# Chunk attention in pairs of heads, with matmuls on alternating row and column halves of TensorE

## The chip, the cores and the metric

The kernel runs on one core of one Trainium2 chip. The metric is the device time of one execution in microseconds (us); lower is better. The time of the kernel before is the median of three executions. A profile of one further execution is what is read below.

## The reference

The reference is a streaming encoder trunk of two layers over 512 tokens of width 1024: an S5/DeltaNet mixer, cross-attention and a SwiGLU network in layer 0; a chunk attention, cross-attention and SwiGLU in layer 1. The change touches the chunk attention alone:

```python
def chunk_attention(h, w_qkv, w_out, q_g, k_g, rel_bias):     # 16 heads of 64, CHUNK = 64
    qkv = (h @ w_qkv).reshape(bsz, seq, 3, CA_HEADS, CA_HEAD_DIM)
    q, k, v = rms_norm(qkv[:, :, 0], q_g), rms_norm(qkv[:, :, 1], k_g), qkv[:, :, 2]
    ...
    def one_chunk(c):      # 64 queries against their own chunk and the 8 chunks before it
        s = jnp.einsum('bqhd,bkhd->bhqk', q_c, k_c) * scale + bias     # bias: learned, by distance
        s = jnp.where((band_pos + start) >= 0, s, -1e30)
        p = jax.nn.softmax(s, axis=-1)
        return jnp.einsum('bhqk,bkhd->bqhd', p, v_c)
    ...
    return o @ w_out
```

With 512 tokens the band covers everything before a query, so it is attention that is causal by chunks of 64.

## The kernel before

One hand-written instruction stream per engine; semaphores alone order them. Tokens lie in four tiles of 128 rows (TT = 4, P = 128). The large products take each f32 operand as a high and a low part (three matmuls, lines 310 to 312); chunk attention itself works on plain f32. One f32 matmul of the program appears in the trace as two matmul instructions; a transpose appears as one.

Query and key are held transposed (`cqT`, `ckT`) with two heads to a 128-row block: head h lies in rows 64*(h % 2) to 64*(h % 2) + 63 of block h // 2. Head by head, for the four row blocks i of queries with n = 128*(i + 1) keys each (1280 columns a head):

- **scores** (`ca_scores_pe`, L1763): a matmul on 64 rows of the array, into PSUM bank i;
- **sums** (in `ca_dve`, L1846): DVE adds the bias from a ring of four tiles (`bias_ring`, loaded by `ca_sp`), writes `p_c` and takes the row maximum; L1850 negates the maxima. L1840 first writes -1e30 into a 64x64 corner of the bias tile (the mask);
- **exps** (L1823): ACT exponentiates the four row blocks with their sums;
- **rescale** (L1861, L1864): DVE takes the reciprocals of the sums and scales the four row blocks;
- **turn** (`ca_turn_p_pe`, L1773): TensorE transposes p, key block s of all row blocks into one of the three PSUM banks 4 to 6 in rotation, ten transposes a head;
- **copy** (`ca_copy`): out of those banks into `pT_c`; s = 0 and 3 by ACT (L1795), s = 1 and 2 by DVE (L1797);
- **values** (`ca_values_pe`, L1782): v times p transposed into 64 partitions (a column half of the array) of bank 7;
- **out_hi, out_lo** (L1833 on ACT, L1855 on DVE): bank 7 split into the high and low part of the output, 64 partitions each.

TensorE's order is turn(h), scores(h + 2), values(h); DVE's is out_lo(h - 1), two copies, rescale(h + 1), sums(h + 2); ACT's is two copies, exps(h + 1), out_hi(h). After the last out_lo comes the output projection (L310). In the code below `link` and `after` are helpers that count semaphores.

Of the kernel before, what the change touches and what calls it, by code (L numbers as in the profile page):

```python
# [5 lines left out]
F32 = mybir.dt.float32  # L6
# [5 lines left out]
P = 128  # L12
# [58 lines left out]
def build_program(nc, A):  # L71
    ctx = ExitStack()
    with ctx:
# [9 lines left out]
        with nc.sbuf_tensor("params", [P, N_PAR], F32) as par:  # L83
# [999 lines left out]
        LEVELS = 5  # L1083

        def solve_start_pool(g):

            for i in range(TT):
# [589 lines left out]
        c_max, c_neg, c_sum, c_rec = cs(2, TT), cs(2, TT), cs(2, TT), cs(2, TT)  # L1677
        ck_rows = rows(high_b)
        cqT, ckT = feat(high_c), feat(high_d)
        p_c = [reg(arena + 2048 * n, TT, SEQ) for n in range(2)]  # L1680
        pT_c = [reg(at_b + 2048 * n, TT, SEQ) for n in range(2)]
        c_oT = hT


# [69 lines left out]
        def ca_scores_pe(pe, h):
            r = slice(64 * (h % 2), 64 * (h % 2) + 64)
            if h == 0:
# [8 lines left out]
        def ca_turn_p_pe(pe, h):  # L1765
            for s in range(TT):
                m = 4 * h + s
                if m >= 3:
                    pe.wait_ge(sem(COPY[(m - 3) % 4][0]), 2 * ((m - 3) // 4) + COPY[(m - 3) % 4][1])
# [6 lines left out]
        def ca_values_pe(pe, h):
            r = slice(64 * (h % 2), 64 * (h % 2) + 64)
            if h > 0:
                pe.wait_ge(sem("c_ol"), h)
            for s in range(TT):  # L1780
                pe.wait_ge(sem(COPY[s][0]), 2 * h + COPY[s][1])
                ins = pe.matmul(ps[r, 7, s * P:SEQ], v_rows[:, s, h * CD:(h + 1) * CD], pT_c[h % 2][:, s, s * P:SEQ],  # L1782
                                start=(s == 0), stop=(s == TT - 1), skip_group_check=True)
            ins.then_inc(sem("c_o"), 1)


        COPY = [("c_pa", 1), ("c_pv", 1), ("c_pv", 2), ("c_pa", 2)]

        def ca_copy(eng, h, s):
            eng.wait_ge(sem("c_tr"), 4 * h + s + 1)  # L1790
            if h >= 2:
                eng.wait_ge(sem("c_o"), h - 1)
            dst, src = pT_c[h % 2][:, s, s * P:SEQ], ps[:, 4 + (4 * h + s) % 3, s * P:SEQ]
            if COPY[s][0] == "c_pa":
                eng.activation(dst, src, ACT.Copy).then_inc(sem("c_pa"), 1)  # L1795
            else:
                eng.tensor_copy(dst, src).then_inc(sem("c_pv"), 1)  # L1797

        def ca_pe(pe):

            ca_scores_pe(pe, 0)
            ca_scores_pe(pe, 1)
            for h in range(CH):
                ca_turn_p_pe(pe, h)
                if h + 2 < CH:
                    ca_scores_pe(pe, h + 2)
                ca_values_pe(pe, h)

        def ca_sp(sp, h):
            if h == 0:  # L1810
                sp.wait_ge(sem("c_rows"), 1)
            if h >= 4:
                sp.wait_ge(sem("c_s2"), 4 * (h - 3))
            e = A["rel_rows"]
            src = bass.AP(e.tensor, h * BAND_E, [[1, P], [1, BAND_W]])
            sp.dma_start(bias_ring[:, h % 4, :], src).then_inc(sem(f"bias_in{h % 4}"), 16)

        def ca_act(a):
            def exps(h):
                a.wait_ge(sem("c_max"), h + 1)  # L1820
                for i in range(TT):
                    n = (i + 1) * P
                    a.activation(p_c[h % 2][:, i, 0:n], p_c[h % 2][:, i, 0:n], ACT.Exp, bias=c_neg[:, h % 2, i:i + 1],  # L1823
                                      accum_out=c_sum[:, h % 2, i:i + 1]).then_inc(sem("c_exp"), 1)
            exps(0)
            for h in range(CH):
                ca_copy(a, h, 0)
                ca_copy(a, h, 3)
                if h + 1 < CH:
                    exps(h + 1)  # L1830
                a.wait_ge(sem("c_o"), h + 1)
                r = slice(64 * (h % 2), 64 * (h % 2) + 64)
                a.activation(c_oT[0][r, h // 2, :].rearrange("p (i n) -> p i n", i=TT),  # L1833
                                  ps[r, 7, :].rearrange("p (i n) -> p i n", i=TT)[:, :, ::-1], ACT.Copy).then_inc(sem("c_oc"), 1)

        def ca_dve(v):
            def sums(h):
                v.wait_ge(sem(f"bias_in{h % 4}"), after(f"bias_in{h % 4}", 16 * (h // 4 + 1)))

                link(v, v.memset(bias_ring[64:P, h % 4, BAND_W - 64:BAND_W], -1e30), "dve_step")  # L1840
                if h >= 2:
                    v.wait_ge(sem("c_tr"), 4 * (h - 1))
                for i in range(TT):
                    n = (i + 1) * P
                    v.wait_ge(sem("c_s"), 4 * h + i + 1)
                    v.tensor_tensor_reduce(out=p_c[h % 2][:, i, 0:n], in0=ps[:, i, 0:n],  # L1846
                                                in1=bias_ring[:, h % 4, BAND_W - n:BAND_W], scale=1.0, scalar=-3.0e38,
                                                op0=ALU.add, op1=ALU.max, accum_out=c_max[:, h % 2, i:i + 1]).then_inc(sem("c_s2"), 1)
                v.wait_ge(sem("c_s2"), 4 * h + 4)
                v.tensor_scalar(c_neg[:, h % 2, :], c_max[:, h % 2, :], -1.0, None, ALU.mult).then_inc(sem("c_max"), 1)  # L1850

            def out_lo(h):
                r = slice(64 * (h % 2), 64 * (h % 2) + 64)
                v.wait_ge(sem("c_oc"), h + 1)
                v.tensor_tensor(c_oT[1][r, h // 2, :].rearrange("p (i n) -> p i n", i=TT),  # L1855
                                ps[r, 7, :].rearrange("p (i n) -> p i n", i=TT)[:, :, ::-1],
                                c_oT[0][r, h // 2, :].bitcast(F32).rearrange("p (i n) -> p i n", i=TT), ALU.subtract).then_inc(sem("c_ol"), 1)

            def rescale(h):
                v.wait_ge(sem("c_exp"), 4 * h + 4)  # L1860
                link(v, v.reciprocal(c_rec[:, h % 2, :], c_sum[:, h % 2, :]), "dve_step")  # L1861
                for i in range(TT):
                    n = (i + 1) * P
                    v.tensor_scalar(p_c[h % 2][:, i, 0:n], p_c[h % 2][:, i, 0:n], c_rec[:, h % 2, i:i + 1], None, ALU.mult).then_inc(sem("c_p"), 1)  # L1864
# [4 lines left out]
            for h in range(CH):
                if h > 0:  # L1870
                    out_lo(h - 1)
                ca_copy(v, h, 1)
                ca_copy(v, h, 2)
                if h + 1 < CH:
                    rescale(h + 1)
                if h + 2 < CH:
                    sums(h + 2)
            out_lo(CH - 1)
# [54 lines left out]
        def _(pe):  # L1933
# [37 lines left out]
            for l in range(DEPTH):  # L1971
# [153 lines left out]
        def _(g):  # L2125
# [78 lines left out]
```

## Time and profile before

| what | value |
|---|---|
| time, median of 3 runs (lowest to highest) | 1906.85 us (1906.24 to 1907.49) |
| the profiled execution: its own time / its span | 1907.66 us / 1905.9 us |
| mean granted TensorE clock, share of full | 0.96 |
| busy over the span: PE, DVE, ACT, POOL | 92%, 43%, 33%, 13% |
| the attention loop (1187.3 to 1297.2 us), busy: PE, DVE, ACT, POOL | 103.5, 79.4, 59.1, 0 of 109.9 us |
| TensorE instructions in that loop | 408 |

Instruction rows give a start, a duration, the engine (PE is TensorE, DVE VectorE, ACT ScalarE, POOL GpSimd), the line, the operation, what it writes and reads, shapes, and a count where rows are merged; in brackets stands the idle time before it and what ended it. A shape as 64*128 in a PE row is the rows and columns of the array in use. Matmuls are pipelined, so a merged row of n matmuls lasts from the first start to the last end, and the time of one is the distance between starts. The granted clock is 1.00 at 2.4 GHz and 0.50 at 1.2 GHz.

### The profile page before, as it was taken

The numbers are of one execution on the slowest core, as the hardware profiler recorded it, in microseconds if no ns is written. First come the engines' busy times: TensorE is split into PE (matmuls) and PEld (weight loads), VectorE is DVE, ScalarE is ACT, GpSimd is POOL, SyncE is SP. The second block draws the span as 40 slices with busy tenths as digits, with TensorE's granted clock in tenths as the row PEclk, the third lists the DMA queues.
The fourth block names the chain that finished last, engine by engine and source line by source line (L and its number), as shares of the span: only waits on it lengthen the run. The fifth ranks groups of instructions, "written<-read, shape, count | busy, mean of one in ns | idle before, by whom it ended". The sixth has DMA issues, their size and how long they took to land.

```text
span 1905.9 us, 20683 instructions
## 1 busy us (share of the span) xinstructions
PE 1762.2 (92%) x8392; PEld 1437.8 (75%) x8392; DVE 811.7 (43%) x1054; ACT 629.5 (33%) x998; POOL 238.8 (13%) x285
## 2 busy tenths in 40 slices
PE   6997585999998999999998999999998999999998
PEld 5877565987775788888887887557876778888887
DVE  5844554445535333333214353673545243333212
ACT  5222054224534333223114234453434233222210
POOL 1782003330000011111000000000000001111000
PEclk9997677999999999999999999899999999999999
DMA  6215001022420233332232231121431133333321
GB/s 197 89 39 95 0 1 45 1 67 88 155 89 23 66 84 92 89 109 88 97 102 89 75 120 53 37 72 45 162 104 44 48 86 88 97 101 88 105 94 67
DMA packets 146795, 151.97 MB, mean 80 GB/s; under 512 B 8864, under 2 KB 109344, under 8 KB 146592
## 3 DMA queue, kind: packets, MB, share of 16 engines
q1 hardware_dynamic: 146720, 150.92, 26.0%
q8 instruction: 53, 0.87, 0.2%
q14 instruction: 22, 0.18, 0.0%
HBM read 147.76 MB, written 3.15 MB: 79 GB/s over the span
## 4 chain that ended last, share of the span: by engine, by line
PE 85%; DVE 9%; ACT 3%; issue 2%; DMA 0%; POOL 0%; SPq 0%; DVEq 0%; ACTq 0%
PE ps L310 22%; PE ps L311 22%; PE ps L312 22%; PE ps L1763 2%; PE ps L1782 2%; PE ps L1504 2%; PE ps L1481 1%; PE ps L384 1%; PE ps L1121 1%; PE ps L1131 1%; PE ps L895 1%; PE ps L1136 1%; DVE sb L348 1%; PE ps L836 1%; PE ps L738 1%
## 5 line engine op out<-in xcount | busy, mean ns | idle before, releaser
L310 PE MATMUL ps<-h_hi,w_hi 128*128 128x512 f32 x864 | 337.2, 390 | 3.3 <-DVE w_lo_ab L282 3.3
L311 PE MATMUL ps<-h_lo,w_hi 128*128 128x512 f32 x864 | 336.8, 390 | 0.0
L282 DVE TENSOR_TENSOR w_lo<-raw,w_hi 128x2048 fp32r<-128x2048 f32 x70 | 160.4, 2292 | 408.1 <-ACT w_hi L278 408.1
L278 ACT ACTIVATE w_hi<-raw 128x2048 fp32r<-128x2048 f32 x84 | 160.6, 1913 | 430.6 <-PE ps L312 429.5
L312 PE MATMUL ps<-h_hi,w_lo 128*128 128x512 f32 x704 | 273.9, 389 | 0.0
L310 PE MATMUL ps<-w_hi,h_hi 128*128 128x512 f32 x512 | 199.8, 390 | 6.5 <-DVE h_lo L1557 2.8
L311 PE MATMUL ps<-w_lo,h_hi 128*128 128x512 f32 x512 | 199.2, 389 | 0.0
L312 PE MATMUL ps<-w_hi,h_lo 128*128 128x512 f32 x512 | 199.2, 389 | 0.0
L310 PEld LDWEIGHTS ps<-h_hi,w_hi 128*128 128x128 f32 x864 | 162.5, 188 | 37.6 <-DVE w_lo_ab L282 3.8
L311 PEld LDWEIGHTS ps<-h_lo,w_hi 128*128 128x128 f32 x864 | 162.6, 188 | 33.5
L1639 POOL CAST a_hi<-up 128x512 f32 x44 | 27.0, 614 | 1213.3 <-DVE up L1627 1213.3
L1629 DVE TENSOR_TENSOR w_lo<-raw,w_hi 128x2048 fp32r<-128x2048 f32 x44 | 140.6, 3194 | 52.2 <-ACT w_hi L1615 52.2
L312 PEld LDWEIGHTS ps<-h_hi,w_lo 128*128 128x128 f32 x704 | 132.2, 188 | 27.3
L1615 ACT ACTIVATE w_hi<-raw 128x2048 fp32r<-128x2048 f32 x44 | 84.4, 1918 | 197.2 <-PE ps L312 197.2
L1627 DVE TENSOR_TENSOR up<-up,ps 128x512 f32<-128x512 f32 x44 | 30.3, 688 | 262.3 <-PE ps L312 262.3
L310 PE MATMUL ps<-w_hi,a_hi 128*128 128x512 f32 x352 | 137.2, 390 | 1.8 <-DVE up L1627 1.8
L311 PE MATMUL ps<-w_lo,a_hi 128*128 128x512 f32 x352 | 136.9, 389 | 0.0
L312 PE MATMUL ps<-w_hi,a_lo 128*128 128x512 f32 x352 | 136.9, 389 | 0.0
L310 PEld LDWEIGHTS ps<-w_hi,h_hi 128*128 128x128 f32 x512 | 96.1, 188 | 28.8 <-DVE h_lo L1557 4.5
L312 PEld LDWEIGHTS ps<-w_hi,h_lo 128*128 128x128 f32 x512 | 96.1, 188 | 20.0
L311 PEld LDWEIGHTS ps<-w_lo,h_hi 128*128 128x128 f32 x512 | 96.1, 188 | 19.6
L310 PEld LDWEIGHTS ps<-w_hi,a_hi 128*128 128x128 f32 x352 | 66.1, 188 | 16.3 <-DVE up L1627 2.6
(331 smaller groups left out, 2551.7 us busy)
## 6 DMA issues: line engine op xcount, KB each, us to landing
raw<-in_f_w_gate SPq DMA_DIRECT2D x44, 512.0 KB, 4.0
raw<-in_f_w_up SPq DMA_DIRECT2D x44, 512.0 KB, 5.3
raw<-in_f_w_down SPq DMA_DIRECT2D x44, 512.0 KB, 4.2
raw<-in_xa_w_kv SPq DMA_DIRECT2D x16, 1024.0 KB, 5.0
raw<-in_c_w_qkv SPq DMA_DIRECT2D x12, 1024.0 KB, 5.0
raw<-in_ab_w_in SPq DMA_DIRECT2D x10, 1024.0 KB, 5.4
raw<-in_xa_w_q SPq DMA_DIRECT2D x8, 1024.0 KB, 5.0
raw<-in_xa_w_out SPq DMA_DIRECT2D x8, 1024.0 KB, 5.0
```

Source lines behind the costliest of these rows:

```text
L278: a.activation(w_hi[:, n % 2, :], raw[n % 2], ACT.Copy).then_inc(sem("w_hi"), 1)
L282: v.tensor_tensor(w_lo(n)[:, n % 2, :], raw[n % 2], w_hi[:, n % 2, :].bitcast(F32), ALU.subtract).then_inc(sem("w_lo"), 1)
L310: pe.matmul(out, a[0], b[0], start=start, stop=False)
L311: pe.matmul(out, a[0], b[1], start=False, stop=False)
L312: return pe.matmul(out, a[1], b[0], start=False, stop=stop)
L1504: ins = pe.matmul(ps[:, 6 + d, :], xv[:, s, h * XD + d * P:h * XD + (d + 1) * P], pT_x[h % 2][:, s, :], start=(s == 0), stop=(s == 1))
L1615: a.activation(w_hi[:, slot, :], raw[slot], ACT.Copy).then_inc(sem("w_hi"), 1)
L1627: v.tensor_tensor(prod[:, s, :], gsil[:, s, :], ps[:, 4 * s + 1, :], ALU.mult).then_inc(sem(f"f{l}_free"), 1)
L1629: v.tensor_tensor(w_lo(n0)[:, slot, :], raw[slot], w_hi[:, slot, :].bitcast(F32), ALU.subtract).then_inc(sem("w_lo"), 1)
L1639: g.tensor_copy(aT[0][:, at], prod[:, s, :]).then_inc(sem(f"f{l}_ahi"), 1)
L1763: pe.matmul(ps[:, i, 0:n], cqT[r, h // 2, i * P:(i + 1) * P], ckT[r, h // 2, 0:n], start=True, stop=True).then_inc(sem("c_s"), 1)
L1782: ins = pe.matmul(ps[r, 7, s * P:SEQ], v_rows[:, s, h * CD:(h + 1) * CD], pT_c[h % 2][:, s, s * P:SEQ], start=(s == 0), stop=(s == TT - 1) ...
```

## The change

Heads are taken in pairs m (heads 2m and 2m + 1, e = 0 and 1). Scores alternate between the row halves, head e in bank + e; values alternate between the column halves of bank 7. The row blocks go in the order 3, 2, 0, 1, and block 1 reuses the banks of block 3, so it waits for the sums of block 3. The next pair's scores wait for all sums of the pair before. DVE still scales all row blocks; out_hi and out_lo take the pair in one instruction of 128 partitions; a negation serves a pair. The mask moves to GpSimd (`ca_pool`). ACT interleaves its exps with its copies. `pT_c` has one buffer per half instead of one of two per head; `p_c` has two per half.

```diff
+        CA_ROWS, CA_EXP = (3, 2, 0, 1), (3, 2, 1, 0)
+        def ca_score(i, e):
+            bank, c0 = {3: (0, 0), 2: (2, 0), 0: (2, 3 * P), 1: (0, 0)}[i]
+            return ps[:, bank + e, c0:c0 + (i + 1) * P]
...
-        def ca_scores_pe(pe, h):
-            r = slice(64 * (h % 2), 64 * (h % 2) + 64)
...
-            for i in range(TT):
-                if h > 0:
-                    pe.wait_ge(sem("c_s2"), 4 * (h - 1) + i + 1)
-                n = (i + 1) * P
-                pe.matmul(ps[:, i, 0:n], cqT[r, h // 2, i * P:(i + 1) * P], ckT[r, h // 2, 0:n], start=True, stop=True).then_inc(sem("c_s"), 1)
+        def ca_scores_pe(pe, m):
...
+            else:
+                pe.wait_ge(sem("c_s2"), 8 * m)
+            for n, i in enumerate(CA_ROWS):
+                if n == 3:
+                    pe.wait_ge(sem("c_s2"), 8 * m + 2)
+                for e in range(2):
+                    r = slice(64 * e, 64 * e + 64)
+                    ins = pe.matmul(ca_score(i, e), cqT[r, m, i * P:(i + 1) * P], ckT[r, m, 0:(i + 1) * P], start=True, stop=True)
+                ins.then_inc(sem("c_s"), 1)
...
+        def ca_values_pe(pe, m):
+            if m > 0:
+                pe.wait_ge(sem("c_ol"), m)
             for s in range(TT):
+                for e in range(2):
+                    pe.wait_ge(sem(COPY[2 * s + e][0]), 4 * m + COPY[2 * s + e][1])
+                    h = 2 * m + e
+                    ins = pe.matmul(ps[64 * e:64 * e + 64, 7, s * P:SEQ], v_rows[:, s, h * CD:(h + 1) * CD], pT_c(e, s),
+                                    start=(s == 0), stop=(s == TT - 1), skip_group_check=True)
             ins.then_inc(sem("c_o"), 1)
...
-        COPY = [("c_pa", 1), ("c_pv", 1), ("c_pv", 2), ("c_pa", 2)]
+        COPY = [("c_pa", 1), ("c_pv", 1), ("c_pa", 2), ("c_pv", 2), ("c_pv", 3), ("c_pa", 3), ("c_pv", 4), ("c_pa", 4)]
...
+            for m in range(CH // 2):
+                ca_turn_p_pe(pe, m)
+                if m + 2 < CH // 2:
+                    ca_scores_pe(pe, m + 2)
+                ca_values_pe(pe, m)
...
         def ca_act(a):
+            for m in range(CH // 2):
+                if m + 1 < CH // 2:
+                    a.wait_ge(sem("c_max"), m + 2)
+                for e in range(2):
+                    for j in range(4):
+                        if m + 1 < CH // 2:
+                            exp(m + 1, e, CA_EXP[j])
+                        n = 4 * e + j
+                        if COPY[n][0] == "c_pa":
+                            ca_copy(a, m, n)
+                a.wait_ge(sem("c_o"), m + 1)
...
         def ca_dve(v):
             sums(0)
             sums(1)
-            rescale(0)
-            for h in range(CH):
+            rescale(0, 0)
+            rescale(0, 1)
+            for m in range(CH // 2):
+                if m > 0:
+                    out_lo(m - 1)
+                for n in range(8):
+                    if COPY[n][0] == "c_pv":
+                        ca_copy(v, m, n)
+                    if n == 4 and m + 1 < CH // 2:
+                        rescale(m + 1, 0)
+                if m + 2 < CH // 2:
+                    sums(m + 2)
+                if m + 1 < CH // 2:
+                    rescale(m + 1, 1)
+            out_lo(CH // 2 - 1)
```

TensorE, scores and values of the first round, before (L1763 scores of head 2, L1782 values of head 0):

```order
L1763 MATMUL ps<-sb 128x128 [waits c_s2]
L1763 MATMUL ps<-sb 128x256 [waits c_s2]
L1763 MATMUL ps<-sb 128x384 [waits c_s2]
L1763 MATMUL ps<-sb 128x512 [waits c_s2]
L1782 MATMUL ps<-sb 64x512 [waits c_pa]
```

The same place now (L1779 scores of pair 2, L1801 values of pair 0; c_s2 counts sums done, c_pa and c_pv the copies of ACT and DVE):

```order
L1779 MATMUL ps<-sb 128x512 [waits c_s2]
L1779 MATMUL ps<-sb 128x512
L1779 MATMUL ps<-sb 128x384 x2
L1779 MATMUL ps<-sb 128x128 x2
L1779 MATMUL ps<-sb 128x256 [waits c_s2]
L1779 MATMUL ps<-sb 128x256
L1801 MATMUL ps<-sb 64x512 [waits c_pa]
L1801 MATMUL ps<-sb 64x512 [waits c_pv]
```

Each matmul has its twin of the other half right behind it, and the block of 256 keys now stands behind a second wait for sums, with all values of the round behind it.

DVE in the same round, now (L1819 copies, L1885 and L1889 rescale(1, 0), L1871 sums(2); ISA is the sum with maximum; the names sv_yc and sv_mask are semaphores that serve as c_rec and c_mask):

```order
L1819 COPY sb<-ps 128x256 [waits c_tr]
L1885 RECIPROCAL sb<-sb 128x4 [waits c_exp]
L1889 TENSOR_SCALAR sb<-sb 128x512 [waits sv_yc]
L1889 TENSOR_SCALAR sb<-sb 128x384
L1889 TENSOR_SCALAR sb<-sb 128x256
L1889 TENSOR_SCALAR sb<-sb 128x128
L1819 COPY sb<-ps 128x128 [waits c_tr]
L1871 ISA sb<-ps,sb 128x512 [waits c_s,c_tr,sv_mask]
```

Before, the same stretch of a head ran:

```order
L1797 COPY sb<-ps 128x256 [waits c_tr]
L1861 RECIPROCAL sb<-sb 128x4 [waits c_exp]
L1864 TENSOR_SCALAR sb<-sb 128x128 [waits dve_step]
...
L1840 MEMSET sb 64x64 [waits x_tile2]
L1846 ISA sb<-ps,sb 128x128 [waits c_s,c_tr,dve_step]
```

The memset is gone from DVE, and the sums of the block of 512 keys, on which TensorE's second wait rests, stand behind a rescale that waits for exps.

## Rows read from the trace of the kernel before

**Rows 1.** Windows: busy us (count) of PE, PEld, DVE, ACT, POOL; clock; DMA share, GB/s.

```profile
576.50:617.00 40.50, 33.07 (x136) 21.97 (x134) 21.36 (x26) 17.71 (x47) 0.00 (x0) 1.00 0.08 26
1175.60:1182.70 7.10, 7.10 (x65) 6.91 (x63) 5.25 (x7) 5.65 (x9) 0.00 (x0) 1.00 0.01 2
1187.20:1204.20 17.00, 15.07 (x31) 7.54 (x32) 9.92 (x42) 5.33 (x18) 0.00 (x0) 0.50 0.16 40
1218.60:1231.10 12.50, 12.19 (x53) 6.76 (x52) 9.86 (x37) 7.23 (x23) 0.00 (x0) 1.00 0.16 43
```

**Rows 2.** The chain that ended last, two heads: start, us, what.

```profile
1218.15 0.61 ACT sb L1795
...
1219.13 2.35 PE ps L1763 x8
1221.48 2.31 PE ps L1782 x8
...
1230.69 0.61 ACT sb L1795
```

**Rows 3.** Timeline of PE: S5 matmuls on alternating column halves.

```profile
177.92 3.95 PE L789 MATMUL ps<-sb 128*64 128x64 f32 x128 [1.18 <-ACT memT L972]
```

**Rows 4.** Timeline of PE where S5's output matmuls pass from one row half to the other.

```profile
227.65 0.63 PE L837 MATMUL ps<-sb 64*64 64x128 f32 x2
228.07 0.69 PE L836 MATMUL ps<-sb 64*64 64x128 f32 x4
228.50 0.69 PE L837 MATMUL ps<-sb 64*64 64x128 f32 x4
228.99 0.63 PE L836 MATMUL ps<-sb 64*64 64x128 f32 x2
```

**Rows 5.** Timeline of ACT, head 2.

```profile
1217.56 0.59 ACT L1833 ACTIVATE h_hi<-ps 64x512 fp32r<-64x512 f32 x1 [2.20 <-PE ps L1782]
1218.15 0.60 ACT L1795 ACTIVATE sb<-ps 128x512 f32<-128x512 f32 x1
...
1219.34 0.39 ACT L1823 ACTIVATE sb<-sb 128x128 f32<-128x128 f32 x1
...
1220.81 0.71 ACT L1823 ACTIVATE sb<-sb 128x512 f32<-128x512 f32 x1
1221.42 0.19 ACT L1823 ACTIVATION_READ_ACCUMULATOR sb<-sb 128x1 f32 x1
```

**Rows 6.** Timeline of DVE: rescale, out_lo and copies of a head.

```profile
1209.11 0.18 DVE L1861 RECIPROCAL sb<-sb 128x4 f32<-128x4 f32 x1 [1.99 <-ACT sb L1823]
1209.32 1.27 DVE L1864 TENSOR_SCALAR sb<-sb 128x128 f32<-128x128 f32 x4
...
1212.78 0.69 DVE L1855 TENSOR_TENSOR h_lo<-ps,h_hi 64x512 fp32r<-64x512 f32 x1
1213.51 0.89 DVE L1797 COPY sb<-ps 128x384 f32<-128x384 f32 x2
```

**Rows 7.** Timeline of DVE: mask and sums of head 0.

```profile
1187.23 0.11 DVE L1840 MEMSET sb<- 64x64 f32 x1
1187.37 0.29 DVE L1846 CUSTOM_DVE_ANT_0 sb<-ps,sb 128x128 f32<-128x128 f32 x1
...
1188.41 0.69 DVE L1846 CUSTOM_DVE_ANT_0 sb<-ps,sb 128x512 f32<-128x512 f32 x1
...
1189.14 0.17 DVE L1850 TENSOR_SCALAR sb<-sb 128x4 f32<-128x4 f32 x1
```

**Rows 8.** Timeline of PE: scores of heads 0 and 1, first projection matmul after the loop.

```profile
1183.68 2.39 PE L1763 MATMUL ps<-sb 64*128 64x128 f32 x8 [0.94 <-DVE sb L1751]
1187.73 4.63 PE L1763 MATMUL ps<-sb 64*128 64x128 f32 x8 [1.65 <-DVE sb L1846]
...
1297.22 0.50 PE L310 MATMUL ps<-w_hi,h_hi 128*128 128x512 f32 x1 [1.41 <-DVE h_lo L1855]
```

**Rows 9.** DMA issues from 1150 to 1297 us: KB each, median us to landing.

```profile
sb<-in_rel_rows SPq DMA_DIRECT2D x12, 256.0 KB, 3.3
```

More of the change, by code:

```diff
@@ L45 @@
 BAND_W = SEQ
+LEVELS = 5
 BAND_E = BAND_W + P - 1
@@ L105, in build_program @@
                    "cat_hi": ("go_sq", TT), "cat_lo": ("go_n", TT), "mem_kept": ("cat_s5", 1),
+                   "c_pv2": ("sv_u", LEVELS * TT),
+                   "c_mask": ("sv_mask", LEVELS * TT), "c_rec": ("sv_yc", LEVELS * TT),
                    "s5_pad": ("conv", 12), "y_v": ("conv", 20), "y_a": ("u_s", 4)}
@@ L1080, in gdn_prod_dve @@
                 v.tensor_tensor(dst[:, i], ps[:, bank, :].rearrange("p (a b) -> p a b", a=GH), dec_m, ALU.mult).then_inc(sem("g_at"), 1)
-        LEVELS = 5
         def solve_start_pool(g):
@@ L1676, in build_program, with p_c, pT_c @@
         c_ss, c_rt, c_r = cs(2, CH // 2), cs(2, CH // 2), cs(2, CH // 2)
-        c_max, c_neg, c_sum, c_rec = cs(2, TT), cs(2, TT), cs(2, TT), cs(2, TT)
+        c_max, c_neg, c_sum, c_rec = cs(2, 2, TT), cs(2, 2, TT), cs(2, 2, TT), cs(2, 2, TT)
         ck_rows = rows(high_b)
         cqT, ckT = feat(high_c), feat(high_d)
-        p_c = [reg(arena + 2048 * n, TT, SEQ) for n in range(2)]
-        pT_c = [reg(at_b + 2048 * n, TT, SEQ) for n in range(2)]
+        CA_ROWS, CA_EXP = (3, 2, 0, 1), (3, 2, 1, 0)
+        CA_TRI = P * TT * (TT + 1) // 2
+        def p_c(m, e, i):
+            at = arena + (2 * (m % 2) + e) * CA_TRI + P * (i * (i + 1) // 2)
+            return reg(at, (i + 1) * P)
+        def pT_c(e, s):
+            at = arena + (4 + e) * CA_TRI + P * (s * TT - s * (s - 1) // 2)
+            return reg(at, (TT - s) * P)
+        def ca_score(i, e):
+            bank, c0 = {3: (0, 0), 2: (2, 0), 0: (2, 3 * P), 1: (0, 0)}[i]
+            return ps[:, bank + e, c0:c0 + (i + 1) * P]
         c_oT = hT
@@ L1751, in ca_turn_evac @@
                     eng.tensor_scalar(dst, src, scale, None, ALU.mult).then_inc(sem("c_Tv"), 1)
[L1754 to L1756 removed]
+        def ca_scores_pe(pe, m):
+            if m == 0:
                 pe.wait_ge(sem("c_Ta"), 8)
                 pe.wait_ge(sem("c_Tv"), 8)
[L1759 to L1763 removed]
@@ L1765, in ca_turn_p_pe @@
[L1765 to L1769, printed above, removed]
+            else:
[7 more added lines that the diff above has]
+                ins.then_inc(sem("c_s"), 1)
@@ L1770, in ca_turn_p_pe @@
+        def ca_turn_p_pe(pe, m):
+            for n in range(8):
+                s, e = n // 2, n % 2
+                g = 8 * m + n
+                if g >= 3:
+                    pe.wait_ge(sem(COPY[(g - 3) % 8][0]), 4 * ((g - 3) // 8) + COPY[(g - 3) % 8][1])
                 for i in range(s, TT):
                     if s == 0:
-                        pe.wait_ge(sem("c_p"), 4 * h + i + 1)
-                    ins = pe.transpose(ps[:, 4 + m % 3, i * P:(i + 1) * P], p_c[h % 2][:, i, s * P:(s + 1) * P], ident)
+                        pe.wait_ge(sem(RESCALE[i][0]), after(RESCALE[i][0], RESCALE[i][1] * (2 * m + e) + RESCALE[i][2]))
+                    ins = pe.transpose(ps[:, 4 + g % 3, i * P:(i + 1) * P], p_c(m, e, i)[:, s * P:(s + 1) * P], ident)
@@ L1774, in ca_turn_p_pe @@
                 ins.then_inc(sem("c_tr"), 1)
[L1776 to L1779, printed above, removed]
+        def ca_values_pe(pe, m):
+            if m > 0:
+                pe.wait_ge(sem("c_ol"), m)
             for s in range(TT):
-                pe.wait_ge(sem(COPY[s][0]), 2 * h + COPY[s][1])
-                ins = pe.matmul(ps[r, 7, s * P:SEQ], v_rows[:, s, h * CD:(h + 1) * CD], pT_c[h % 2][:, s, s * P:SEQ],
-                                start=(s == 0), stop=(s == TT - 1), skip_group_check=True)
-            ins.then_inc(sem("c_o"), 1)
@@ new lines, in ca_values_pe, with ca_copy @@
+            ins.then_inc(sem("c_o"), 1)
+        COPY = [("c_pa", 1), ("c_pv", 1), ("c_pa", 2), ("c_pv", 2), ("c_pv", 3), ("c_pa", 3), ("c_pv", 4), ("c_pa", 4)]
+        RESCALE = [("c_pv2", 4, 4), ("c_pv2", 4, 3), ("c_pv2", 4, 2), ("c_pv2", 4, 1)]
+        def ca_copy(eng, m, n):
+            s, e = n // 2, n % 2
+            g = 8 * m + n
+            eng.wait_ge(sem("c_tr"), g + 1)
+            if m >= 1:
+                eng.wait_ge(sem("c_o"), m)
+            dst, src = pT_c(e, s), ps[:, 4 + g % 3, s * P:SEQ]
+            if COPY[n][0] == "c_pa":
@@ L1812, in ca_sp @@
             if h >= 4:
-                sp.wait_ge(sem("c_s2"), 4 * (h - 3))
+                sp.wait_ge(sem("c_s2"), 8 * (h // 2 - 1))
             e = A["rel_rows"]
@@ L1818, in ca_act @@
         def ca_act(a):
[L1819 to L1834, printed above, removed]
@@ L1836, in ca_dve @@
-        def ca_dve(v):
[L1837 to L1864, printed above, removed]
@@ new lines, in exp @@
+            def exp(m, e, i):
+                p = p_c(m, e, i)
+                a.activation(p, p, ACT.Exp, bias=c_neg[:, m % 2, e, i:i + 1], accum_out=c_sum[:, m % 2, e, i:i + 1]).then_inc(sem("c_exp"), 1)
+            a.wait_ge(sem("c_max"), 1)
+            for e in range(2):
+                for i in CA_EXP:
+                    exp(0, e, i)
+            for m in range(CH // 2):
+                if m + 1 < CH // 2:
+                    a.wait_ge(sem("c_max"), m + 2)
+                for e in range(2):
+                    for j in range(4):
+                        if m + 1 < CH // 2:
+                            exp(m + 1, e, CA_EXP[j])
+                        n = 4 * e + j
+                        if COPY[n][0] == "c_pa":
+                            ca_copy(a, m, n)
+                a.wait_ge(sem("c_o"), m + 1)
+                a.activation(c_oT[0][:, m, :].rearrange("p (i n) -> p i n", i=TT),
+                                  ps[:, 7, :].rearrange("p (i n) -> p i n", i=TT)[:, :, ::-1], ACT.Copy).then_inc(sem("c_oc"), 1)
@@ new lines, in ca_dve, with sums, out_lo, rescale @@
+        def ca_dve(v):
+            def sums(m):
+                v.wait_ge(sem("c_mask"), after("c_mask", 2 * m + 2))
+                if m >= 2:
+                    v.wait_ge(sem("c_tr"), 8 * (m - 1))
+                for n, i in enumerate(CA_ROWS):
+                    v.wait_ge(sem("c_s"), 4 * m + (1, 3, 3, 4)[n])
+                    for e in range(2):
+                        v.tensor_tensor_reduce(out=p_c(m, e, i), in0=ca_score(i, e),
+                                                    in1=bias_ring[:, (2 * m + e) % 4, BAND_W - (i + 1) * P:BAND_W], scale=1.0, scalar=-3.0e38,
+                                                    op0=ALU.add, op1=ALU.max, accum_out=c_max[:, m % 2, e, i:i + 1]).then_inc(sem("c_s2"), 1)
+                v.wait_ge(sem("c_s2"), 8 * m + 8)
+                v.tensor_scalar(c_neg[:, m % 2], c_max[:, m % 2], -1.0, None, ALU.mult).then_inc(sem("c_max"), 1)
+            def out_lo(m):
+                v.wait_ge(sem("c_oc"), m + 1)
+                v.tensor_tensor(c_oT[1][:, m, :].rearrange("p (i n) -> p i n", i=TT),
+                                ps[:, 7, :].rearrange("p (i n) -> p i n", i=TT)[:, :, ::-1],
+                                c_oT[0][:, m, :].bitcast(F32).rearrange("p (i n) -> p i n", i=TT), ALU.subtract).then_inc(sem("c_ol"), 1)
+            def rescale(m, e):
+                v.wait_ge(sem("c_exp"), 8 * m + 4 * e + 4)
+                v.reciprocal(c_rec[:, m % 2, e], c_sum[:, m % 2, e]).then_inc(sem("c_rec"), 1)
+                v.wait_ge(sem("c_rec"), after("c_rec", 2 * m + e + 1))
+                for i in (3, 2, 1, 0):
+                    p = p_c(m, e, i)
+                    v.tensor_scalar(p, p, c_rec[:, m % 2, e, i:i + 1], None, ALU.mult).then_inc(sem("c_pv2"), 1)
@@ L1866, in ca_dve @@
             sums(0)
             sums(1)
-            rescale(0)
[L1869 to L1878, printed above, removed]
+            rescale(0, 0)
[3 more added lines that the diff above has]
+                    out_lo(m - 1)
+                for n in range(8):
+                    if COPY[n][0] == "c_pv":
[6 more added lines that the diff above has]
+                    rescale(m + 1, 1)
@@ L1881, in load_panel, with ca_pool, mask @@
+            out_lo(CH // 2 - 1)
+        def ca_pool(g):
+            def mask(m):
+                for h in (2 * m, 2 * m + 1):
+                    g.wait_ge(sem(f"bias_in{h % 4}"), after(f"bias_in{h % 4}", 16 * (h // 4 + 1)))
+                    g.memset(bias_ring[64:P, h % 4, BAND_W - 64:BAND_W], -1e30).then_inc(sem("c_mask"), 1)
+            for m in range(CH // 2):
+                mask(m)
+            g.wait_ge(sem("c_mask"), after("c_mask", CH))
         def load_panel(sp, name):
@@ L1993, in _ @@
                     ca_pe(pe)
-                    pe.wait_ge(sem("c_ol"), CH)
+                    pe.wait_ge(sem("c_ol"), CH // 2)
                     split_outproj_pe(pe, "co", cao, c_oT)
@@ L2133, in _ @@
             ffn_up_pool(g, 0)
+            ca_pool(g)
             ffn_up_pool(g, 1)
```

10 lines of the change are left out of this document (removed).

## Prediction

> **What bounds the kernel now.** I first looked at the windows of the attention loop. For two heads they show 12.5 us in which TensorE is busy for 12.19, DVE for 9.86, ACT for 7.23 and GpSimd for nothing, at full clock [rows 1]. So TensorE is nearly closed and DVE has a fifth to spare. The chain of waits says the same: in a head it is 2.35 us of scores and 2.31 us of values, and only one ACT copy of 0.61 us among transposes is not TensorE [rows 2]. The same ACT copy recurs after two heads at 1230.69 against 1218.15, a period of 12.54 us. The remaining part of it is the 20 transposes: 65 of them filled 7.10 us, 0.109 us each [rows 1], so 2.2 us, plus waits between them.
>
> What the reader should note is what those 4.66 us per head do. Scores use 64 of 128 rows, values 64 of 128 columns. The change runs the two heads' halves beside each other. Whether the hardware overlaps them is the first question, and the S5 part of this very kernel answers it.
>
> **Do the halves overlap?** A transpose of 128 columns takes 0.109 us, so one matmul instruction of 64 columns alone would take 0.055. In the S5 states, whose matmuls alternate between the column halves, 128 instructions of 64 columns take 3.95 us, less the last one's tail some 0.030 us each [rows 3]. That is 1.8 to 1.9 times faster. For rows there is one place: S5's output runs all matmuls of row half 0 and then those of half 1. Within a half two instructions (one matmul) take 228.07 - 227.65 = 0.42 us, at half clock. Where the half changes, eight take 228.99 - 228.07 = 0.92 instead of 1.7 us, again 1.85 times faster [rows 4]. Both places have short matmuls. None of 512 columns alternates, so the bounds for the pair are once to twice the rate; I take twice, since the loss at both places is a fixed few ns per instruction and these are four to eight times longer. Then scores of a pair take 2.35 us (before 4.7) and values 2.31 (before 4.62), 4.65 us off TensorE.
>
> **What then sets the period.** TensorE needs 2.2 + 2.35 + 2.31 and some 0.3 for changes of shape, 7.2 us a pair. DVE: sums 2 x 1.77 (first sum to negation, 1187.37 to 1189.14) plus one negation 0.2, out_lo once at 0.73 (to the next start; the same columns on 128 partitions), four copies of the same 1280 columns 1.75 (before 2 x 0.89), rescales 2 x 1.5 [rows 6, 7]: 9.2 us. Saved there are two memsets with their waits (0.14 each), one out_lo (0.73) and a negation (0.2). ACT needs 7.0: exps 2 x 2.27 (1219.34 to the end of the last read, 1221.61), copies 1.8, out_hi 0.6 [rows 5]. None of these is the answer, since the new order ties them in a loop. Let 0 be the end of values(m - 1).
>
> ACT: out_hi to 0.65; then in its order exp of 512 keys (0.71), copy of 512 (0.60), exp 384 (0.60), exp 256 (0.50), copy 384 (about 0.50, between those of 512 and 128), exp 128 (0.39), done at 3.95. The 384 and 256 are read off between the 0.39 and 0.71 shown, at 0.10 a block. DVE's rescale(m + 1, 0) waits for this: 3.95 + 1.5 = 5.45. Behind it on DVE, in order, stand the copy of 128 (0.25, 5.7) and the two sums of block 3 (0.61 each from start to start, and a wait: 7.0). TensorE's second wait in the scores holds block 1 until then; block 1 takes 0.43 and 0.2 to refill, values(m) begin at 7.6 and end at 9.95. **The period is 9.95 us**, 2.6 less than now.
>
> Checks on what is assumed done: DVE's rescale(m, 1) ends at about 1.2, out_lo at 1.9, its copies at 2.5, 3.1 and 3.5. The transposes, held at times by these copies and by ACT's second one (3.45), end at 3.95. Scores of block 3 are then ready at 5.2, before DVE wants them at 5.7. After 7.0 DVE has 2.1 us of sums, 0.2 and the rescale of 1.5 left, 10.9, or 1.0 behind the end of values, which is the 1.2 I began with. So DVE has hardly 0.7 us of idle time per pair and TensorE some 2.7.
>
> **The ends.** DVE is free at 1187.23 as before [rows 7]. Sums(0) end at 1190.6, since block 1 has to wait for block 3. Scores(1) begin there. At half clock, as now (4.63 against 2.39 us for one head [rows 8]), block 3 is ready at 1192.7 and sums(1) end at 1196.9. The rescales end at 1198.45 and 1199.95, two copies and rescale(1, 0) at 1204.8, sums of block 3 at 1207.1, block 1 at 1208.1. Values(0) end at 1210.5 at full or 1212.9 at half clock; I take 1211. Then five periods: 1260.8. The last two pairs have no scores: values(6) follow at once on the transposes (3.95 + 0.15 + 2.35, +6.5). For pair 7 rescale(7, 1) ends at +7.2, out_lo(6) at +7.95, DVE's copies at +9.5, values(7) end at +12.15, out_hi and out_lo at +13.5: 1274.3. Now the projection starts at 1297.22 [rows 8]. **The sum is -22.9 us**, 1907.66 - 22.9 = 1884.8 against the profiled execution; that one lies 0.8 above the median, so I say 1884.5.
>
> **Costed at nothing.** The 16 masks go to GpSimd, idle in this loop [rows 1]. A bias tile is asked for when sums(m) are done and wanted 16 us later (9.95 + 6). It lands in 3.3 us [rows 9], so a mask, 0.11 us on DVE, may take several us on GpSimd unseen; without that cover its time would come on top of every pair. The bias issues move ahead in SP's queue with the sums, and the weights of the second projection half behind them with them. Nothing after the loop changes; TensorE bounds it.
>
> **Rivals.**
> *Halves overlap, but at about 1.5 instead of 2.* Against it are the 1.85 of rows 3 and 4; for it, that long matmuls read twice the data at once. Values +0.8, block 1 +0.15, so +0.95 on eight rounds: 1892.
> The Trainium skill, "TensorE: Matmul & The Clock Gate", Measured speedup vs the span model, gives 2.38 for three column tiles; an estimate from that page for two is 1.6. The rows say 1.85.
>
> *Only row halves overlap.* Values stay at 4.6: +2.3 on eight rounds, 1903. Rows 3 are against it.
>
> *No overlap at all.* Period: block 3 ready at 6.05, sums to 7.35, but TensorE only reaches block 1 at 7.6, 8.5, values to 13.3. Five rounds +16.8, two last pairs +4.7, start +3: 1909, about as now.
>
> *The clock falls (the other side).* TensorE would idle 2.7 of 9.95 us, mostly among transposes. It runs 17 us at half clock at the start of the loop now, where it is busy 15.07 of 17 with half-row matmuls among waits [rows 1]. Against it: cross-attention held full clock busy 33.07 of 40.5 us, and 7.10 us of transposes alone held it [rows 1]; both halves together are more work per us than now. If it falls, transposes end at 4.8, DVE's rescale at 6.0, block 1 is done at 9.3 and values end at 14.3, above today's 12.54: five rounds +21.8, last pairs +6.5, start +2: 1915. The case costs 30.3 us on top of the sum, so it ends slower than now once the clock is half for over three quarters of the rounds (22.9 of 30.3).
> The Trainium skill, same page, PE-mode transpose, says that transposes do not count as busy for the clock; by it the transposes of 4 us a round would lose the clock and give this 1915. The trace disagrees: 65 transposes in 7.10 us at clock 1.00.
>
> **How the numbers follow.** Full overlap at kept clock 0.76, overlap at 1.5 0.08, rows only 0.04, none 0.04, clock falls 0.08. The first gives the time. Its own range: DVE's 9.2 as the period (-3.8 for five rounds) and no half clock at the start (-4) give 1877; half clock through the first values and 0.3 of added waits a round give 1889. With the 1.5 case and the same additions: 1877 to 1895. No change that a measurement of this kernel can tell is within 0.2%, 3.8 us. Faster: 0.76 + 0.08 + half of rows only, 0.86; same: the other half, and none: 0.06; slower 0.08.
>
> **What would show it.** In the profile after: pairs of L1801 and L1779 starting together, eight 2-instruction matmuls of values in 2.4 us rather than 4.6; a period near 9.95; DVE busy over 85% in the loop; the chain passing from ACT's exp of 128 through rescale, copy and the first sums to the block-1 scores and values; clock 1.00 after the first rounds; L310 at about 1274. Wrong would be: starts of the two halves one after the other, a clock below 1.00 past 1215, DVE waiting for a mask, or a chain that sits on DVE alone.

## The result, and the profile after

The changed kernel takes 1883.59 us (median of 4 runs, 1881.87 to 1884.16) against 1906.82 us (4 runs, 1906.24 to 1907.49): ratio 0.9877, 95% interval 0.9859 to 0.9894, 23.2 us less. The forecast was 1884.5 us, 1877 to 1895.

The page of the profile after, its first lines:

```profile
span 1881.9 us, 20643 instructions
...
PE 1725.4 (92%) x8392; PEld 1420.8 (75%) x8392; DVE 802.1 (43%) x1022; ACT 621.9 (33%) x990; POOL 240.9 (13%) x301
```

TensorE runs as many instructions as before in less busy time, with the same share. The average over the whole program hides the change; the windows of the loop show it (columns as in [rows 1]):

```profile
1187.30:1272.50 85.20, 65.86 (x404) 38.49 (x404) 70.55 (x257) 51.47 (x169) 2.01 (x13) 0.94 0.20 63
...
1229.38:1239.05 9.67, 7.89 (x53) 4.55 (x54) 8.74 (x33) 6.23 (x21) 0.29 (x2) 1.00 0.18 54
```

A round of two heads takes 9.67 us instead of the 12.54 of [rows 2]. TensorE is busy for 7.89 of them where it was for 12.19 of 12.5 [rows 1]; DVE, at 8.74, is now the fullest engine, yet it too is idle for 0.9 us. No engine is full, so the period must come from a chain of waits that closes on itself over several engines: a loop. TensorE's timeline shows one round:

```profile
1226.33 0.70 PE L1779 MATMUL ps<-sb 64*128 64x256 f32 x4 [0.74 <-DVE sb L1871]
1226.96 2.38 PE L1801 MATMUL ps<-sb 128*64 128x512 f32 x16
1229.26 0.66 PE L1791 MATMUL ps<-sb 128*128 128x128 f32 x4
...
1231.22 0.77 PE L1791 MATMUL ps<-sb 128*128 128x128 f32 x5 [0.18 <-ACT sb L1817]
1232.68 0.66 PE L1791 MATMUL ps<-sb 128*128 128x128 f32 x4 [0.69 <-ACT sb L1817]
1233.27 2.00 PE L1779 MATMUL ps<-sb 64*128 64x512 f32 x12
```

Sixteen instructions of values, two heads, take 2.38 us; eight of one head took 2.31 [rows 2]. Sixteen of scores take 2.0 + 0.7. So the halves overlap in full. What ends TensorE's three larger waits is DVE's sums ahead of block 1 (0.74) and ACT's copies amid the transposes (0.69 and 0.18).

The chain of waits over one round (start, us, what):

```profile
1219.71 0.03 ACT h_hi L1860
...
1220.20 0.11 ACT sb L1843
...
1222.58 0.38 ACT sb L1817
1222.95 0.39 ACT sb L1843 x2
...
1223.37 0.19 DVE sb L1885
...
1223.98 0.84 DVE sb L1889 x3
...
1224.97 1.31 DVE sb L1871 x4
...
1226.33 0.70 PE ps L1779 x4
1227.03 2.33 PE ps L1801 x16
...
1229.38 0.03 ACT h_hi L1860
```

It is the loop of the prediction: out_hi, exps and copies on ACT, rescale and the first sums on DVE, block 1 and values on TensorE, and out_hi again. The masks, 0.146 us each on GpSimd and 16 of them, are nowhere on it.

The two ends of the loop, from the chain's first sum and TensorE's timeline:

```profile
1187.64 3.38 DVE sb L1871 x16
```

```profile
1272.56 0.50 PE L313 MATMUL ps<-w_hi,h_hi 128*128 128x512 f32 x1 [1.42 <-DVE h_lo L1879]
```

From the first sum to the projection it is 84.9 us, where it was 1297.22 - 1187.37 = 109.85 [rows 7, 8]: 24.9 less.

### The profile page after: what moved, and what is told of

Same layout as the page of the kernel before. It is cut to its first block, busy times and chain, and to the rows that moved or that the text cites. A ratio compares the mean times of both kernels' runs of the same rounds, so it can differ in the third digit from the quotient of the medians.

```text
span 1881.9 us, 20643 instructions
## 1 busy us (share of the span) xinstructions
PE 1725.4 (92%) x8392; PEld 1420.8 (75%) x8392; DVE 802.1 (43%) x1022; ACT 621.9 (33%) x990; POOL 240.9 (13%) x301
## 4 chain that ended last, share of the span: by engine, by line
PE 83%; DVE 10%; ACT 3%; issue 2%; DMA 0%; POOL 0%; SPq 0%; DVEq 0%; ACTq 0%
PE ps L313 22%; PE ps L315 22%; PE ps L314 22%; PE ps L1482 2%; PE ps L1505 2%; PE ps L387 1%; PE ps L1122 1%; PE ps L1132 1%; PE ps L1801 1%; PE ps L898 1%; PE ps L1137 1%; DVE sb L351 1%; PE ps L741 1%; PE ps L839 1%; DVE sb L1871 1%
```

## The experiments

"Loop" below is from the first sum to the first projection matmul (84.9 after, 109.85 before); "rest" from there to the end of the span; "round" the distance of two out_hi on ACT. All three are read from each kernel's profiled execution. What the table leaves out, the time before the first sum, lies between 1185.8 and 1188.5 us.

| kernel | round | loop | rest | median us (runs) |
|---|---|---|---|---|
| before | 12.53 (two heads) | 109.8 | 608.7 | 1906.82 (4) |
| changed | 9.67 | 84.9 | 609.4 | 1883.59 (4) |
| changed, again | 9.67 | 84.9 | 609.4 | 1884.01 (4) |
| rows_one | 10.88 | 95.8 | 609.0 | 1893.31 (3) |
| cols_one | 11.81 | 101.1 | 607.2 | 1896.65 (3) |
| both_one | 13.02 | 112.0 | 609.4 | 1909.17 (8) |
| mask_on_dve | 10.17 | 87.1 | 607.2 | 1884.40 (2) |
| scores_by_head | 10.57 | 91.6 | 607.7 | 1887.43 (1) |
| values_by_head | 11.22 | 96.4 | 608.8 | 1894.00 (1) |
| values_by_twos | 9.71 | 85.2 | 609.2 | 1882.57 (2) |
| exp_before_out | 9.07 | 81.3 | 607.8 | 1877.66 (4) |
| exp_before_out, again | 9.07 | 81.3 | 607.8 | 1877.84 (5) |
| exp_before_and_copy | 9.06 | 81.8 | 609.2 | 1878.77 (4) |

### Is the gain the overlap? One half for both heads

Rows:

```diff
-                    r = slice(64 * e, 64 * e + 64)
+                    r = slice(0, 64)
```

> This kernel sends the scores of both heads of a pair through rows 0 to 63 of the array (head 2m twice, so that part of the output is not the reference's). Theory A, the row halves overlap in the changed kernel and a loop values, out_hi, exps, rescale, sums of block 3, scores of block 1 sets the period of 9.67 us: scores of a pair take 4.7 us instead of 2.3, block 3 comes 0.6 us later than DVE wants it, TensorE reaches block 1 at 7.4 us and is done with it at 8.5 instead of 7.3, so the period is 10.8 us and the time about 1891 us. Rival B, the gain is DVE's shorter list and the halves do not matter: period 9.7, time 1884.

Columns:

```diff
-                    ins = pe.matmul(ps[64 * e:64 * e + 64, 7, s * P:SEQ], v_rows[:, s, h * CD:(h + 1) * CD], pT_c(e, s),
+                    ins = pe.matmul(ps[0:64, 7, s * P:SEQ], v_rows[:, s, h * CD:(h + 1) * CD], pT_c(e, s),
```

> This kernel writes the values of both heads of a pair into partitions 0 to 63, one column half (head 2m's values are overwritten, the output is not the reference's). Theory A: values of a pair take 4.6 us instead of 2.33, all of it on the loop, period 12.0 us, eight rounds of 2.3 us, time about 1902 us. Rival B: DVE's list sets the period and TensorE's idle 2 us take most of it up: period below 10.5, time below 1889.

Both edits:

> Both of the two edits together: scores through rows 0 to 63, values into partitions 0 to 63 (output not the reference's). Theory A: no overlap left, period 13.0 to 13.3 us against 12.54 of the kernel before, time about 1909 us, so all of the gain is overlap. Rival B: time stays under 1890 us. If the regrouping in pairs has a gain of its own, the time is below 1906.

rows_one and both_one leave out the scores of head 2m + 1 and compute those of head 2m twice; in cols_one and both_one the values of head 2m are overwritten. These kernels serve for the time alone.

Rounds of 10.88, 11.81 and 13.02 us (expected 10.8, 12.0, 13.0 to 13.3), medians of 1893.31, 1896.65 and 1909.17 (expected 1891, 1902, 1909). The median of cols_one is 5 us under the expected one: its loop grew by 16.2 us and not by 18.4, and the rest and the start before the first sum came out 3.7 shorter. TensorE's timeline, scores in rows_one and values in cols_one:

```profile
1230.51 4.65 PE L1779 MATMUL ps<-sb 64*128 64x512 f32 x16
```

```profile
1229.72 4.52 PE L1801 MATMUL ps<-sb 128*64 128x512 f32 x16
```

The same sixteen instructions, 2.0 + 0.7 and 2.38 us in opposite halves, take nearly twice as long when they share a half. In both_one the chain is TensorE again:

```profile
1232.18 4.58 PE ps L1779 x16
1236.76 4.46 PE ps L1801 x16
...
1241.25 0.03 ACT h_hi L1860
```

That kernel has everything of the change but the overlap, and takes 1909.17 us against 1907.10 of the kernel before on that chip (ratio 1.0010, 0.9998 to 1.0021). So the whole gain needs the overlap; the regrouping by itself gains nothing, and may cost up to 4 us. Rival B, DVE's shorter list, falls.

### Where the loop runs: the mask back on DVE

```diff
-                v.wait_ge(sem("c_mask"), after("c_mask", 2 * m + 2))
+                for h in (2 * m, 2 * m + 1):
+                    v.wait_ge(sem(f"bias_in{h % 4}"), after(f"bias_in{h % 4}", 16 * (h // 4 + 1)))
+                    link(v, v.memset(bias_ring[64:P, h % 4, BAND_W - 64:BAND_W], -1e30), "dve_step")
```

> The mask goes back from GpSimd to DVE, two memsets of 0.14 us from start to start, ahead of the sums of block 3 and so on the loop. Theory A: period 9.95 instead of 9.67, time about 1.7 us longer than the changed kernel. Rival B, DVE's idle 0.7 us of a round (two waits) hides them: period 9.67.

The round is 10.17, 0.5 us longer, and not 9.67: DVE's idle time does not hide work that stands on the loop. It is also more than the 0.28 of two memsets. DVE's timeline shows why (without the mask the sum starts 0.20 after the copy, 1224.97 - 1224.77):

```profile
1225.57 0.28 DVE L1819 COPY sb<-ps 128x128 f32<-128x128 f32 x1
1225.92 0.30 DVE L1867 MEMSET sb<- 64x64 f32 x2
1226.25 0.69 DVE L1873 CUSTOM_DVE_ANT_0 sb<-ps,sb 128x512 f32<-128x512 f32 x1
```

From copy to sum it is 0.68 us: each instruction here starts only after its forerunner's end, where without the mask the sum starts before the copy has ended. The memsets stand behind semaphore waits, and they write partitions 64 to 127 alone, where their neighbours write all 128; which of the two costs the extra 0.2 us no run separates. The time hardly moved (1884.40), as the rest came out at 607.2 instead of 609.4; the loop is 2.2 longer. The changed kernel has a stretch of 3.4 us at half clock, 158 us behind the start of the projection, which this one has not; it can account for 1.7 of the 2.2 us by which the rest is shorter.

### How far apart may the twins stand?

Values by head, all of one and then all of the other; scores of blocks 3, 2 and 0 likewise; and values in twos:

```diff
-            for s in range(TT):
-                for e in range(2):
+            for e in range(2):
+                for s in range(TT):
```

> All values of head 2m stand ahead of all of head 2m + 1, in opposite column halves, so the twins are four matmuls apart in the program. Theory A1, each half has its own stream and takes work that stands up to four matmuls ahead, as at the change of row halves in the S5 part of the kernel before (two matmuls ahead): values still take about 2.4 us, time 1884. Rival A2, matmuls start in program order and only neighbours overlap: values take 4.5 us, period about 11.8, time about 1901.

```diff
+            for part in ((3, 2, 0), (1,)):
+                if part == (1,):
                     pe.wait_ge(sem("c_s2"), 8 * m + 2)
                 for e in range(2):
                     r = slice(64 * e, 64 * e + 64)
+                    for i in part:
```

> Scores of blocks 3, 2, 0 of head 2m stand ahead of those of head 2m + 1 (three matmuls apart), block 1 as before. A1, own streams: the three blocks take 1.8 us, block 3 ready as now, period 9.67, time 1884. A2, program order: block 3 of head 2m + 1 ready only at 3.9 + 1.7 + 0.9 = 6.5 us against 5.3 wanted, period about 10.8, time about 1890.

```diff
+            for e, s in ((0, 0), (0, 1), (1, 0), (1, 1), (0, 2), (0, 3), (1, 2), (1, 3)):
```

> Values in twos: blocks 0 and 1 of head 2m, blocks 0 and 1 of head 2m + 1, then blocks 2 and 3 of each. In the two kernels ordered by head, the second stream began just when only four matmul instructions (two matmuls) of the first were not yet past. If that distance is the rule here, the twins start together again at a distance of two matmuls: values 2.4 us, period 9.67, time as the changed kernel. If only neighbours overlap fully: each two of the four twos runs alone for about a matmul, values above 3 us, period above 10.3.

TensorE's timeline, one round's values by head, scores by head, values in twos:

```profile
1229.34 3.93 PE L1801 MATMUL ps<-sb 128*64 128x512 f32 x16
```

```profile
1225.25 2.96 PE L1780 MATMUL ps<-sb 64*128 64x512 f32 x12
```

```profile
1225.13 2.42 PE L1801 MATMUL ps<-sb 128*64 128x512 f32 x16
```

Neither first expectation held: 3.93 us lies between 2.4 and 4.5, and 2.96 between 2.0 and 4. But both fit one distance. Two short windows of values by head, around 1230.8 and 1231.1 us, show where head 2m + 1 joins in:

```profile
1230.57 0.49 PE L1801 MATMUL ps<-sb 128*64 128x384 f32 x1
```

```profile
1230.89 0.65 PE L1801 MATMUL ps<-sb 128*64 128x256 f32 x2
```

Up to 1230.89, 1.55 us from the start, one half runs alone: these are head 2m's two matmuls of 512 and 384 columns, and 3.93 - 2.38 is 1.55 as well. Then head 2m + 1 starts together with head 2m's matmul of 256 columns. In the scores it is 0.96 us, the first of three matmuls, and 2.96 - 2.00 is 0.96. In both, the second head starts when two matmuls of the first, four instructions, are still to go, although these are of 256 and 128 columns in one and 384 and 128 in the other. The third kernel was made to test this: twins two matmuls apart, and values take 2.42 us, round 9.71. So the halves need not alternate one by one; here two matmuls apart was near enough, three was not. The two kernels by head ran once each; their rounds are alike to 0.01 us within the run.

### Is it the loop or DVE? The first exp ahead of out_hi

```diff
                         n = 4 * e + j
                         if COPY[n][0] == "c_pa":
                             ca_copy(a, m, n)
+                if m + 2 < CH // 2:
+                    a.wait_ge(sem("c_max"), m + 3)
+                    exp(m + 2, 0, CA_EXP[0])
                 a.wait_ge(sem("c_o"), m + 1)
```

> ACT does the next pair's first exp (512 keys, 0.6 us) before out_hi instead of behind it, in its idle 3.4 us ahead of the end of values. Theory A, the loop through ACT's exps sets the period: exps end 0.6 us earlier, period 9.67 to about 9.07, where DVE's busy 9.06 takes over, five to six rounds, time 3 to 3.6 us below the changed kernel, about 1880.3. Rival C, DVE alone sets the period already: no change.

The round is 9.07 us, as expected; the time is 1877.66 us, 2.6 less than expected (ratio to the kernel before 0.9837, 0.9821 to 0.9854), and this is the fastest kernel here. ACT's timeline: the exp of 512 keys now runs before values end, and out_hi is not late for it.

```profile
1217.72 0.72 ACT L1843 ACTIVATE sb<-sb 128x512 f32<-128x512 f32 x1 [2.65 <-DVE sb L1878]
...
1218.52 0.60 ACT L1863 ACTIVATE h_hi<-ps 128x512 fp32r<-128x512 f32 x1
1219.09 0.60 ACT L1817 ACTIVATE sb<-ps 128x512 f32<-128x512 f32 x1
```

0.60 us taken from one place of the loop shorten the round by 0.60, without a touch to DVE's or TensorE's lists. Rival C falls. The chain shows that the loop is still there, with four transposes (L1791) and the ACT copy behind them in the place of out_hi and the exp:

```profile
1218.47 0.60 PE ps L1791 x4
...
1219.09 0.03 ACT sb L1817
...
1221.57 0.19 DVE sb L1888
...
1223.17 1.31 DVE sb L1874 x4
...
1224.53 0.70 PE ps L1779 x4
1225.23 2.30 PE ps L1801 x16
```

That the round came out at the expectation's "busy 9.06" is chance: that number was DVE's busy time in a window of 10.00 us of the changed kernel, and in a round of 9.67 it was 8.74. But DVE has run out of air as well. In this kernel's round it is busy for 8.79 us, and none of its gaps is longer than 0.08:

```profile
1218.52:1227.58 9.06, 7.94 (x53) 4.58 (x54) 8.79 (x33) 6.42 (x22) 0.29 (x2) 1.00 0.18 57
```

Run again beside the changed kernel on one chip:

> The changed kernel once more, for its spread and beside the next one on the same chip: period 9.67, loop 84.9 us from the first sum to the projection; time 1881.9 to 1884.2.

> The kernel with the earlier exp once more: period 9.07, loop 81.3 us, 3.6 us less than the changed kernel in the loop; medians 3 to 5 us apart. Rival: the 5.9 us between the two medians so far are all the edit's, so that something outside the loop gained 2 us too.

1877.84 against 1884.01. The loops differ by 3.65 us (84.93 and 81.28) and the medians by 6.2, so something outside the loop gained too, as the rival in the last expectation has it: in the profiled executions 1.6 us behind the loop and 1.2 ahead of it. For the 1.6 behind it the windows show where, the norm before the last feed-forward layer, first in the changed kernel, then in exp_before_out:

```profile
1508.67:1515.50 6.83, 6.31 (x29) 5.90 (x29) 6.77 (x9) 4.20 (x7) 0.00 (x0) 0.50 0.35 99
```

```profile
1504.64:1508.00 3.36, 3.00 (x13) 2.71 (x14) 3.36 (x4) 1.68 (x3) 0.00 (x0) 0.50 0.00 0
1508.10:1511.40 3.30, 3.30 (x25) 3.04 (x25) 3.30 (x6) 3.29 (x6) 0.00 (x0) 1.00 0.78 225
```

The same transposes, after the same wait, run for 6.8 us at half clock in one and for 3.4 in the other. Both are so again in the second pair of profiles. It is no merit of the edit: scores_by_head has the short stretch and a rest of 607.7 us without the edit, and exp_before_and_copy has the edit and the long stretch, with a rest of 609.2. What decides between the two stretches no run shows.

### The copy between rescale and sums to ACT

```diff
-        COPY = [("c_pa", 1), ("c_pv", 1), ("c_pa", 2), ("c_pv", 2), ("c_pv", 3), ("c_pa", 3), ("c_pv", 4), ("c_pa", 4)]
+        COPY = [("c_pa", 1), ("c_pv", 1), ("c_pa", 2), ("c_pv", 2), ("c_pv", 3), ("c_pa", 3), ("c_pa", 4), ("c_pa", 5)]
```

> As the kernel with the earlier exp, and the copy of 128 columns that stands between rescale and sums on DVE goes to ACT. Theory A with DVE as the next bound: another 0.2 us a round off both the loop and DVE's list, period about 8.87, time about 1879.2. Rival: ACT's extra copy delays the copies that values wait for, and the time is that of the earlier exp alone or more.

The round stays at 9.06: the expected 0.2 us did not come. The chain, with the copy gone:

```profile
1221.70 0.19 DVE sb L1889
...
1221.92 1.27 DVE sb L1893 x4
...
1223.29 1.32 DVE sb L1875 x4
```

From the reciprocal to the first sum it is 1.59 us; with the copy in between it was 1.60 (1221.57 to 1223.17). The copy had filled a gap that is there anyway. What makes the gap is the scores of block 3. TensorE's four instructions of that block, in rows_one, where the sum plainly waits for them, in exp_before_out and in this kernel:

```profile
1230.51 1.98 PE L1779 MATMUL ps<-sb 64*128 64x512 f32 x4
```

```profile
1221.84 1.13 PE L1779 MATMUL ps<-sb 64*128 64x512 f32 x4
```

```profile
1221.98 1.13 PE L1779 MATMUL ps<-sb 64*128 64x512 f32 x4
```

The first sum in rows_one:

```profile
1232.67 0.69 DVE L1871 CUSTOM_DVE_ANT_0 sb<-ps,sb 128x512 f32<-128x512 f32 x1 [0.69 <-PE ps L1779]
```

There the sum starts 0.18 us after the scores end (1232.67 against 1232.49), which is also the distance in scores_by_head and the shortest in these kernels. In exp_before_out it starts 0.20 after their end (1223.17 against 1222.97) and in this kernel 0.19 (1223.29 against 1223.11). So the copy stood in the way for 0.03 us at most, and the next step for this loop is to bring the scores of block 3 forward. The loop of 81.8 us instead of 81.3 is one round of 9.42; there DVE's first sum comes 0.45 us after its forerunner, and the profile names no releaser.

## Why the prediction was right

**The halves overlap, at twice the rate.** Right: 2.38 us for a pair's values, forecast 2.31; 2.7 for scores with both starts, forecast 2.35. The 1.85 read off short matmuls in rows 3 and 4 does not hold for the longer ones: in one half an instruction of 512 columns starts 0.43 us after the one before it, and in the changed kernel two start every 0.43; at 128 columns it is 0.11 and 0.11. Whether the loss at 64 columns is a fixed one, as was argued, no run tests. The rival at 1.5 and that of rows only are out; with the additions named, the 1.5 case gives 1896 and not the 1895 of the range. "None" was priced at 1909 and measured at 1909.17 by taking the overlap away; its five rounds cost 16.8 us as priced, while the start cost 7.0 instead of 3 and the last pairs 3.4 instead of 4.7.

**The loop sets the period.** Right, and its size is 0.28 too long: 9.95 forecast, 9.67 measured. The terms, from the end of values (1219.71): exp of 128 done at 3.66, forecast 3.95, since ACT's next instruction starts about 0.1 us earlier behind out_hi and behind each of the two copies than was costed (0.49 behind out_hi, 0.38 behind the copy of 384), and the exp of 128 with its read takes 0.1 more (0.49 for 0.39); rescale to the first sum 1.60, forecast 1.75; two sums 1.36, forecast 1.3; block 1 0.70, forecast 0.6; values 2.33, forecast 2.35. Five rounds: -1.4 us.

**The start.** 22.4 us from the first sum to out_hi of pair 0 (1187.64 to 1210.04); forecast 23.8. The first sum came 0.4 us later than the 1187.23 of the forecast, and values(0) ended at 1210.0 instead of 1211: they ran at full clock, as did all TensorE work from 1204.9 on, where the forecast had gone between full (1210.5) and half clock (1212.9). **The end.** 14.2 us from values(5) to the projection, forecast 13.5. There rescale(7, 1) waits for ACT's exps of head 15 until 1264.5 us, 6.1 after values(5); the forecast let it follow at once on the copy of 128, at 5.7, without a look at those exps; this is 0.4 of the 0.7 us.

**The sum.** Forecast -22.9 us for the loop, measured -24.9. The profiled times differ by 23.8 (1907.66 and 1883.86), since the loop begins 0.3 us later than before and the rest is 0.7 us longer. So 1884.5 came this near to 1883.59 with misses that partly cancel: the loop gained 2.0 us more than forecast, and the 1.0 outside it was not foreseen.

**The clock.** It stayed at 1.00 from 1204.9 us to the end of the loop; the rival of the other side did not come. Transposes spread over 4 us of each round did not lower it, against the Trainium skill's remark ("TensorE: Matmul & The Clock Gate", PE-mode transpose) and in line with rows 1.

**DVE's 9.2 us** as the floor of the range was a little high: DVE's list is 8.74 us busy in the changed kernel, and exp_before_out, with 8.79 busy and gaps of 0.08 at most, runs a round in 9.07.

## What to carry to other kernels

In this kernel two matmuls that use 64 rows or 64 columns each took the time of one when they lay in opposite halves and not more than two f32 matmuls apart: look for half-array matmuls of a full-looking TensorE before anything else. Once the fullest engine has air, add up not lists but the loop from a buffer's release to its next, across engines, and move out of it whatever could run before it; here one exp of 0.6 us gave 0.6 us a round. Time such small edits by the round in the trace, since half-clock stretches behind the loop moved the total by 1.6 to 2.2 us, and the start of the loop lay up to 2.8 us apart.

## What the hardware showed beyond that

The stretch of half clock at the start of the loop differed between these kernels. Windows of the 20.7 us from the first sum, of the changed kernel, rows_one and scores_by_head:

```profile
1187.60:1208.30 20.70, 13.64 (x60) 8.30 (x62) 15.77 (x67) 10.44 (x36) 0.58 (x4) 0.75 0.19 51
```

```profile
1188.50:1209.20 20.70, 15.95 (x44) 9.79 (x44) 12.83 (x53) 9.78 (x33) 0.58 (x4) 0.59 0.17 51
```

```profile
1186.25:1206.95 20.70, 14.88 (x52) 9.62 (x52) 13.61 (x55) 10.44 (x36) 0.58 (x4) 0.67 0.17 51
```

In the changed kernel TensorE is busy for less of the time and yet has the higher clock, 0.75 against 0.59 in rows_one; both_one has 0.59 and cols_one has 0.75, but its edit touches the values alone, which begin only as this window ends. The rows in use are not all of it: scores_by_head uses both row halves, with the twins three matmuls apart, and has 0.67. So the clock was the higher the more fully the scores overlapped, but whether the overlap, the rows or the moments at which the matmuls come decide it is not shown. To the first out_hi it is 27.2 us in rows_one and 22.4 in the changed kernel; how the 4.8 us between them divide into clock and missing overlap was not separated.

Also unexpected: one half's matmul starts ahead of earlier ones of the other half that have not begun, up to four instructions back. And the clock can rise on transposes alone: in exp_before_out TensorE runs nothing else from 1503.6 to 1509.8 us, and the clock went from 0.50 to 1.00 at about 1508.05, as the two windows of that kernel above show.
